# Projection phase of a transformer block on one core: output additions ahead of the maxima, other orders in the first steps and between the passes, four Q weight splits by GpSimd

## The chip, the cores and the metric

The kernel runs on one core of a Trainium2 chip. The metric is the device time of one execution in microseconds (us). The kernel before took 2551.72 us in the median of three runs (2550.61, 2551.72 and 2552.01).

## The reference, cut to what matters

The program is one layer of a block with x of 2048 tokens by 1024 features, all in float32. What the changed phase computes is this:

```
h    = rms_norm(x, norm_mix_pre)
proj = h @ w_in                      # 1024 -> 512 + 128 + 128 + 512 + 512 + 512
qa, ka, va, qd, kd, vd = split(proj)
qa, ka, qd, kd = apply_rope(...)     # heads of 64
out_a = swa_sink_attention(qa, ka, va, sinks)   # 8 query heads, 2 key heads, chunks of 64,
                                                # each chunk sees itself and the one before,
                                                # softmax with one sink per head
```

After it come the differential attention of qd, kd and vd over all earlier chunks, the output projection with its norm, and a SwiGLU block of width 2816. Those are not touched.

## The kernel before, in words

The program has three phases with a barrier between them: `proj_phase`, `diff_attn` and `out_proj_and_ffn`. Only `proj_phase` is changed.

The phase walks over tiles of 128 tokens in 33 steps, `i = 0` to `32` (`PASS` is 32, `TILES` is 16). Steps 0 to 15 are the first pass. In it tile i is scaled, turned (transposed), and multiplied by the weights of the windowed attention's Q, of its K and V together ("kv"), and of the differential attention's V ("v"); the windowed attention itself follows tile by tile with a lag. Steps 16 to 31 are the second pass, where the same tiles are turned again and multiplied by the weights of the differential attention's K ("dk") and Q ("dq"). These weights take the place of the first ones in SBUF.

Every float32 operand of a product is split into a high part (rounded, made by ScalarE) and a low part (the rest, made by VectorE), and three products are added: high by high, high by low, low by high. A weight piece is 128 rows of one weight. Pieces 16 to 23 are V's, 24 to 31 dk's and 32 to 39 dq's. `weights_hi` (L473, ScalarE) makes the high part, scaled by the norm's gain, and `weights_lo` (L613, VectorE) the low part out of the raw piece and the high part. SyncE loads a piece when the low part of the piece eight before it is done.

The order of the work is written out by hand: each engine has one instruction stream and takes it strictly in order, and semaphores tie the streams together. In step i of the first pass the streams hold, in this order:

- TensorE: `turn_x(i+1)` (L791); `project` q of tile i (L804); `score(i-1)` (L836); `attend(i-3)` (L860); `project` kv of tile i; `turn_a(i-2)`, first half (L847), the transposes of the probabilities; `turn_q(i)` (L812); `project` v of tile i; `turn_a(i-2)`, second half; `turn_k(i)` (L818).
- VectorE: `turned_lo(i+1)` (L604); `rope_q(i)` (L622, L626); `maxima(i-1)`, which writes the mask with eight memsets (L666; four in tile 0), reduces the scores to maxima (L670) and makes bias and gap (L673 to L676); `add_o(i-3)` (L716, L718, four additions that empty the two output banks); `rope_k(i)`; `scale_x(i+2)` (L598); low parts of the probabilities (L706), of q (L691 to L694) and of k; `recips(i-1)`.
- ScalarE: `turned_hi(i+1)` (L462); `square(i+2)` (L451); `copy_o(i-3)` (L531, L532); `exps(i-1)`, first half (L491), which waits for the gap of L676; `copy_v(i)` (L516), which waits for `rope_k(i)`; high parts of the probabilities (L523) and of q (L500 to L503); `exps(i-1)`, second half; `copy_dv(i)` (L538); the rest.
- GpSimd: `rotate_q(i)` (L387); `split_v(i-2)`; `rotate_k(i)`; `rstd_of(i+2)`; `scale_probs(i-1)` (L408). In the second pass `rotate_d` (L402) takes the place of the rotations.

PSUM has eight banks, and the table `BANK` with `order` says which use follows which in a bank. TensorE waits before it writes into a bank until the use before has been read out. Three entries matter here. kv and v of one tile share bank 6, and kv counts as read out when `copy_v` is done (`"kv": (v_copied, ...)`). The two halves of `attend`'s output stand in banks 5 and 4, and `turn_a`'s first half follows in them when `add_o` is done. Bank 4 holds also q and dk, and `attend`'s second half follows when the rope of q or dk has read them.

Three places have orders of their own. In step 0 the low parts of pieces 16 to 19 come last on VectorE, and in step 1 pieces 20 to 23 come before `rope_k(1)`. In step 1, TensorE runs v of tile 0, `turn_x(2)` and v of tile 1. In step 15 the pieces 24 to 31 are split, and in step 16, before VectorE's rope of dk, the pieces 32 to 39.

Of the kernel before, what the change touches and what calls it, by code (L numbers as in the profile page):

```python
# [22 lines left out]
F32 = mybir.dt.float32  # L23
F32R = mybir.dt.float32r
BF16 = mybir.dt.bfloat16
ALU = mybir.AluOpType
# [7 lines left out]
KC = D // P  # L34
# [133 lines left out]
def proj_phase(nc, x, w_in, g_pre, sinks, rope, swa_t, q_s, k_s, v_s):  # L168
# [7 lines left out]
             [("v", c, WQ, DW) for c in range(KC)]  # L176
    FIRST = {"q": 0, "kv": KC, "v": 2 * KC, "dk": 3 * KC, "dq": 4 * KC}

    order = [("x", 0, 0), ("x", 0, 1)]
# [16 lines left out]
    with ExitStack() as ctx:  # L196
# [45 lines left out]
        w_loaded = [m.sem(f"w_loaded{n}") for n in range(RAW)]  # L242
        w_hi_done, w_lo_done = m.sem("w_hi_done"), m.sem("w_lo_done")
        consts_loaded, consts_made, zeroed = m.sem("consts_loaded"), m.sem("consts_made"), m.sem("zeroed")
# [46 lines left out]
        def attending(t):  # L291
            return 0 <= t < TILES

        with nc.Block() as block:
# [76 lines left out]
            def _(pool):  # L371
# [40 lines left out]
                def split_v(t):  # L412
                    q = t % 2
                    pool.wait_ge(v_copied, t + 1)
                    if t >= 1:
# [5 lines left out]
                        .then_inc(v_split, 1)  # L421

                pool.memset(probs[:, 0, :, P:2 * P], 0.0).then_inc(zeroed, 1)
                pool.memset(probs[:, 1, :, 0:HD], 0.0).then_inc(zeroed, 1)
                rstd_of(0)
                rstd_of(1)
                for i in range(PASS):
                    u = i - TILES
                    if u >= 0:
                        rotate_d("k", u)  # L430
                    else:
                        rotate_q(i)
                    if attending(i - 2):
                        split_v(i - 2)
                    if i < TILES:
                        rotate_k(i)
                    if i + 2 < PASS:
                        rstd_of(i + 2)
                    if attending(i - 1):
                        scale_probs(i - 1)  # L440
                    if u >= 0:
                        rotate_d("q", u)

            @block.scalar
            def _(act):
# [108 lines left out]
                for i in range(PASS + 1):  # L554
                    u = i - TILES
                    if i + 1 < PASS and i != 1:
                        turned_hi(i + 1)
                    if i + 2 < PASS:
                        square(i + 2)
                    if i == TILES - 1:  # L560
                        weights_hi(3 * KC, 4 * KC)
                    if i == TILES:
                        weights_hi(4 * KC, 5 * KC)
                    if attending(i - 3):
                        copy_o(i - 3)
                    if attending(i - 1):
                        exps(i - 1, (0, 1))
                    if i < TILES:
                        copy_v(i)
# [24 lines left out]
            def _(dve):  # L594
# [61 lines left out]
                def maxima(t):  # L656
# [6 lines left out]
                    for j in range(4):  # L663
                        dve.wait_ge(scored, 4 * t + j + 1)
                        for lo, cs in chunks_hidden(t):
                            last = dve.memset(scores(j)[lo:lo + HD, :, cs, :], NEG)  # L666
                        last.then_inc(masked, 1)
                    for j in range(4):
                        dve.wait_ge(masked, 4 * t + j + 1)
                        last = dve.tensor_reduce(top[:, q, 2 * j:2 * j + 2], scores(j)[:, :, chunks_kept(t), :], AX.XY, ALU.max)  # L670
# [63 lines left out]
                for i in range(PASS + 1):  # L734
                    u = i - TILES
                    if i + 1 < PASS and i != 1:
                        turned_lo(i + 1)
                    if i == TILES:
                        weights_lo(4 * KC, 5 * KC)
                    if i < TILES:  # L740
                        rope_q(i)
                    elif i < PASS:
                        rope_d("k", u)
                    if i == 1:
                        weights_lo(5 * KC // 2, 3 * KC)
                        rope_k(i)
                    if attending(i - 1):
                        maxima(i - 1)
                    if i == TILES - 1:
                        weights_lo(3 * KC, 7 * KC // 2)  # L750
                    if attending(i - 3):
                        add_o(i - 3)
                    if i < TILES and i != 1:
                        rope_k(i)
                    if i + 2 < PASS:
                        scale_x(i + 2)
                    if attending(i - 2):
                        lo_a(i - 2, (0, 1))
                    if i < TILES:
                        lo_q(i)  # L760
                    elif u >= 1:
                        lo_d("q", u - 1)
                    if i == TILES - 1:
                        weights_lo(7 * KC // 2, 4 * KC)
                    if attending(i - 1):
# [9 lines left out]
                    elif i < PASS:  # L775
                        lo_d("k", u)
                    if i == 0:
                        weights_lo(2 * KC, 5 * KC // 2)

            @block.tensor  # L780
            def _(pe):
# [13 lines left out]
                def project(n, kind, k, region, width, done):  # L795
                    q = n % 2
                    b = free(kind, k)
                    for c in range(KC):
                        if kind in ("q", "dk") and c % 4 == 0:
                            pe.wait_ge(xt_lo_done, 2 * n + c // 4 + 1)  # L800
                        if k == 0:
                            pe.wait_ge(w_lo_done, FIRST[kind] + c + 1)
                        for j, (lhs, rhs) in enumerate(((xt_hi, w_hi), (xt_hi, w_lo), (xt_lo, w_hi))):
# [1758 lines left out]
```

## Time and profile before

| what | value |
| --- | --- |
| median of 3 runs | 2551.72 us |
| the profiled execution's own time | 2547.37 us |
| its span, first to last instruction | 2545.6 us |
| TensorE busy | 2375.7 us (93%) |
| VectorE busy | 1631.0 us (64%) |
| ScalarE busy | 1202.0 us (47%) |
| GpSimd busy | 682.6 us (27%) |
| mean granted TensorE clock | 0.978 |

Busy time is summed over all stages, so it doesn't tell which wait is worth something; that is read stage by stage. The granted clock is a share of full speed, where 1.00 stands for 2.4 GHz and 0.50 for 1.2 GHz. Matmuls are pipelined, so their shown ends overlap with the start of the next.

### The profile page before, as it was taken

What the parts mean: (1) busy time and instruction counts of PE and PEld (TensorE: products, weight loads), DVE (VectorE), ACT (ScalarE), POOL (GpSimd) and SP (SyncE); (2) the same over time, 40 slices, a digit from 0 to 9 for tenths busy, and PEclk for the clock granted to TensorE, in tenths of its full rate; (3) what the DMA queues carried; (4) which work ended last, traced back from release to release, by engine and by line L of the source; (5) the groups of instructions that cost most, each with busy time, mean ns of one, the idle gap of its engine ahead of it and who ended that gap; (6) DMA issues with size and microseconds to landing.
All of it is one profiled execution on the core that took longest, in us unless ns stands there. A gap on an engine that the chain in (4) does not pass through costs nothing.

```text
span 2545.6 us, 36648 instructions
## 1 busy us (share of the span) xinstructions
PE 2375.7 (93%) x11796; PEld 1978.0 (78%) x11796; DVE 1631.0 (64%) x3093; ACT 1202.0 (47%) x2731; POOL 682.6 (27%) x810
## 2 busy tenths in 40 slices
PE   7999997996888888799999999999999999999997
PEld 5888876885777677577778888888888888888886
DVE  5677776554898888533565545557786565464867
ACT  5555564332666666533453333335454333334444
POOL 1233322221575665445421111110000111111001
PEclk9999998998999999899999999999999999999999
DMA  5111122334232231466663233256674223226773
GB/s 175 47 55 49 52 80 76 135 135 154 74 103 77 72 88 36 161 191 228 204 211 114 96 106 110 78 182 223 229 266 154 100 100 112 100 85 240 240 264 143
DMA packets 222361, 340.08 MB, mean 134 GB/s; under 512 B 20576, under 2 KB 119904, under 8 KB 220384
## 3 DMA queue, kind: packets, MB, share of 16 engines
q1 hardware_dynamic: 222176, 337.86, 39.9%
q8 instruction: 86, 1.41, 0.2%
q14 instruction: 99, 0.81, 0.1%
HBM read 234.50 MB, written 103.28 MB: 133 GB/s over the span
## 4 chain that ended last, share of the span: by engine, by line
PE 52%; DVE 2%; POOL 2%; issue 1%; DMA 1%; ACT 1%; SPq 0%; POOLq 0%; ACTq 0%; DVEq 0%
PE ff_psum L2458 32%; PE ff_psum L2482 16%; PE ff_psum L1736 4%; PE ff_psum L1750 1%; DVE op_y_norm L1665 0%; DMA ff_ring<-in_w_down_dram 0%; DVE op_h_row L1673 0%; POOL op_mt_lo L1521 0%; POOL op_odd L1558 0%; POOL op_odd L1555 0%; ACT op_odd L1620 0%; DMA ff_hop<-hop_s 0%; DMA op_w_raw<-in_w_out_dram 0%; DVE ff_y L2422 0%; DVE ff_a_lo L2215 0%
## 5 line engine op out<-in xcount | busy, mean ns | idle before, releaser
L2458 PE MATMUL ff_psum<-ff_hop,ff_a_hi 128*128 128x512 f32 x2464 | 760.0, 390 | 5.2 <-DVE ff_hop L2222 2.9
L2458 PEld LDWEIGHTS ff_psum<-ff_hop,ff_a_hi 128*128 128x128 f32 x2464 | 462.7, 188 | 102.4 <-issue 6.6
L2458 PE MATMUL ff_psum<-ff_hop,ff_a_lo 128*128 128x512 f32 x1232 | 479.9, 390 | 0.0
L2458 PEld LDWEIGHTS ff_psum<-ff_hop,ff_a_lo 128*128 128x128 f32 x1232 | 231.7, 188 | 48.4
L2482 PE MATMUL ff_psum<-ff_a_hi 128*128 128x512 f32 x616 | 239.8, 389 | 0.3 <-DVE ff_a_lo L2215 0.3
L2482 PE MATMUL ff_psum<-ff_a_hi,ff_a_lo 128*128 128x512 f32 x616 | 239.6, 389 | 0.0
L2482 PE MATMUL ff_psum<-ff_a_lo,ff_a_hi 128*128 128x512 f32 x616 | 239.6, 389 | 0.0
L1221 ACT ACTIVATE da_probs<-da_psum,da_bias 128x512 f32<-128x512 f32 (+3 forms) x320 | 195.9, 621 | 73.6 <-DVE da_bias L1273 60.7
L2088 ACT ACTIVATE ff_a_hi<-ff_w_raw 128x512 fp32r<-128x512 f32 x220 | 137.9, 629 | 193.9 <-PE ff_psum L2458 190.5
L2215 DVE TENSOR_TENSOR ff_a_lo<-ff_w_raw,ff_a_hi 128x512 fp32r<-128x512 f32 x220 | 163.4, 744 | 90.6 <-ACT ff_a_hi L2088 90.6
L2043 POOL TENSOR_TENSOR ff_go<-ff_go 128x512 f32<-128x512 f32 x22 | 28.4, 1291 | 655.2 <-DVE ff_go L2296 635.0
L1267 DVE TENSOR_REDUCE da_tops<-da_psum 128x1 f32<-128x512 f32 (+3 forms) x288 | 173.7, 619 | 26.4 <-PE da_psum L1328 22.0
L2215 DVE TENSOR_TENSOR ff_a_lo<-ff_ring,ff_a_hi 128x512 fp32r<-128x512 f32 x220 | 151.0, 696 | 45.7 <-ACT ff_a_hi L2088 45.7
L2088 ACT ACTIVATE ff_a_hi<-ff_ring 128x512 fp32r<-128x512 f32 x220 | 130.7, 622 | 96.8 <-PE ff_psum L2482 82.5
L1351 PE MATMUL da_psum<-da_values,da_at 128*128 (+1 forms) x1088 | 149.4, 280 | 18.5 <-ACT da_at L1229 10.8
L1351 PEld LDWEIGHTS da_psum<-da_values,da_at 128*128 128x128 f32 x1088 | 138.4, 193 | 34.3 <-issue 19.2
L1328 PE MATMUL da_psum<-da_keys,da_q_hl 128*128 (+3 forms) x320 | 139.9, 440 | 26.0 <-DMA da_keys<-k_s 15.5
L2482 PEld LDWEIGHTS ff_psum<-ff_a_hi 128*128 128x128 f32 x616 | 115.6, 188 | 24.8 <-DVE ff_a_lo L2215 0.7
L2482 PEld LDWEIGHTS ff_psum<-ff_a_lo,ff_a_hi 128*128 128x128 f32 x616 | 115.6, 188 | 24.0
L2482 PEld LDWEIGHTS ff_psum<-ff_a_hi,ff_a_lo 128*128 128x128 f32 x616 | 115.6, 188 | 23.9
L2266 DVE TENSOR_TENSOR ff_s<-ff_psum,ff_s 128x512 f32<-128x512 f32 x66 | 45.6, 691 | 120.8 <-ACT ff_s L2098 84.8
L1328 PE MATMUL da_psum<-da_keys,da_q_lh 128*128 (+3 forms) x320 | 120.3, 378 | 0.0
(230 smaller groups left out, 5000.4 us busy)
## 6 DMA issues: line engine op xcount, KB each, us to landing
g_s<-ff_go SPq DMA_DIRECT2D x154, 256.0 KB, 2.0
ff_ring<-g_s SPq DMA_DIRECT2D x154, 256.0 KB, 2.8
ff_ring<-in_w_down_dram SPq DMA_DIRECT2D x132, 256.0 KB, 3.1
ff_w_raw<-in_w_gate_dram SPq DMA_DIRECT2D x44, 512.0 KB, 3.6
ff_w_raw<-in_w_up_dram SPq DMA_DIRECT2D x44, 512.0 KB, 3.9
pp_x<-in_x_dram SPq DMA_DIRECT2D x32, 512.0 KB, 4.3
ff_hop<-hop_s SPq DMA_DIRECT2D x14, 1024.0 KB, 7.8
hop_s<-op_odd SPq DMA_DIRECT2D x8, 1280.0 KB, 5.5
```

The lines of the kernel that those rows point to most:

```text
L1221: act.activation(probs[:, q, m, 4 * P * c:4 * P * c + w], ps[:, b, 0:w], ACT.Exp, bias=bias[:, r, m:m + 1], accum_out=sums[:, r, m, c:c + ...
L1267: top = dve.tensor_reduce(tops[:, r, m, c:c + 1], ps[:, b, 0:w], AX.X, ALU.max)
L1328: last = pe.matmul(ps[:, b, 0:w], stack[:, s % Q_SLOTS, m, :], keys[:, bass.ds(h, 1), m, 4 * P * c:4 * P * c + w].squeeze(1), start=(j == ...
L1351: last = pe.matmul(ps[:, O_BANK, 0:VD], at[:, n % A_SLOTS, j, :], values[:, bass.ds(h, 1), 4 * c + j, :].squeeze(1), start=(c == 0 and j = ...
L1736: last = pe.matmul(self.ps[:, self.y_banks.bank("y", k, n), :], lhs[:, q, c, :], rhs[n][:, c, :], start=(c == 0 and j == 0), stop=(c == KC ...
L1750: last = pe.transpose(self.ps[:, self.h_bank(k, n), j * P:(j + 1) * P], self.b.op_h_row[:, at:at + P], self.b.op_ident[:, :])
L2043: pool.tensor_tensor(go[:, S1, :], go[:, C12, :], go[:, C22, :], ALU.add).then_inc(go_made, 1)
L2088: act.activation(a_hi[:, n_ % R, :], source, ACT.Copy).then_inc(w_hi_done, 1)
L2215: dve.tensor_tensor(a_lo[:, n_ % R, :], unit_source(n_)[0], a_hi[:, n_ % R, :].bitcast(F32), ALU.subtract)\
L2266: return dve.tensor_tensor(to, ps[:, bank, :], to, ALU.add)
L2458: last = pe.matmul(ps[:, bank, :], w[:, unit % R, at], hop[i][:, h, c, :], start=(i in (0, 1, 6) and c == 0 and x_ == 0), stop=(c == 3 and ...
L2482: last = pe.matmul(ps[:, bank, :], g[:, unit % R, at], w[:, (unit + 1) % R, :], start=(i in (0, 1, 6) and c == 0 and x_ == 0), stop=(c == ...
```

## The change

It has these parts, all in `proj_phase`:

- In `maxima(t)` the additions `add_o(t-2)` now stand between the mask's memsets and the reductions. So they come before the maxima in each step from 3 to 16. In steps 17 and 18 `add_o` stands where it did.
- In step 0 VectorE does `rope_q(0)` before `turned_lo(1)`. All eight V pieces are split in step 1, after `rope_q(1)` and `rope_k(1)`. On ScalarE `copy_v(1)` comes before the exponentials of step 1.
- In step 15 ScalarE makes the high parts of pieces 24 to 27 before `copy_o` and those of 28 to 31 behind it. VectorE does the low parts of 24 to 27 after `rope_k(15)`, and those of 28 to 31 before `lo_q(15)`.
- In step 16 ScalarE makes the high parts of pieces 32 to 39 before `square(18)`. The low parts of 32 to 35 are made by GpSimd (a scaling of the raw piece in place, then a subtraction), ahead of `rotate_d("k", 0)`. VectorE makes those of 36 to 39 after the maxima.

```diff
+    BY_POOL = KC // 2
@@ gpsimd
+                def weights_lo_of_q():
+                    for k in range(BY_POOL):
+                        n = FIRST["dq"] + k
+                        _, c, _, width = pieces[n]
+                        raw = w_raw[:, n % RAW, 0:width]
+                        pool.wait_ge(w_hi_done, n + 1)
+                        pool.tensor_scalar(raw, raw, g_col[:, c:c + 1], 1.0, ALU.mult, ALU.mult).then_inc(w_pool_scaled, 1)
+                        pool.wait_ge(w_pool_scaled, k + 1)
+                        pool.tensor_tensor(w_lo["v"][:, c, 0:width], raw, w_hi["v"][:, c, 0:width].bitcast(F32), ALU.subtract)\
+                            .then_inc(w_pool_lo_done, 1)
...
+                    if i == TILES:
+                        weights_lo_of_q()
                     if u >= 0:
                         rotate_d("k", u)
@@ scalar
                     if i + 1 < PASS and i != 1:
                         turned_hi(i + 1)
+                    if i == TILES:
+                        weights_hi(4 * KC, 5 * KC)
                     if i + 2 < PASS:
                         square(i + 2)
                     if i == TILES - 1:
-                        weights_hi(3 * KC, 4 * KC)
-                    if i == TILES:
-                        weights_hi(4 * KC, 5 * KC)
+                        weights_hi(3 * KC, 7 * KC // 2)
                     if attending(i - 3):
                         copy_o(i - 3)
+                    if i == TILES - 1:
+                        weights_hi(7 * KC // 2, 4 * KC)
+                    if i == 1:
+                        copy_v(i)
                     if attending(i - 1):
                         exps(i - 1, (0, 1))
-                    if i < TILES:
+                    if i < TILES and i != 1:
                         copy_v(i)
@@ maxima
                         last.then_inc(masked, 1)
+                    if attending(t - 2):
+                        add_o(t - 2)
                     for j in range(4):
@@ vector
-                    if i + 1 < PASS and i != 1:
+                    if 1 < i < PASS - 1:
                         turned_lo(i + 1)
-                    if i == TILES:
-                        weights_lo(4 * KC, 5 * KC)
                     if i < TILES:
                         rope_q(i)
                     elif i < PASS:
                         rope_d("k", u)
+                    if i == 0:
+                        turned_lo(1)
                     if i == 1:
-                        weights_lo(5 * KC // 2, 3 * KC)
                         rope_k(i)
+                        weights_lo(2 * KC, 3 * KC)
                     if attending(i - 1):
                         maxima(i - 1)
+                    if attending(i - 3) and not attending(i - 1):
+                        add_o(i - 3)
+                    if i == TILES:
+                        weights_lo(FIRST["dq"] + BY_POOL, 5 * KC)
+                    if i < TILES and i != 1:
+                        rope_k(i)
                     if i == TILES - 1:
                         weights_lo(3 * KC, 7 * KC // 2)
-                    if attending(i - 3):
-                        add_o(i - 3)
-                    if i < TILES and i != 1:
-                        rope_k(i)
                     if i + 2 < PASS:
                         scale_x(i + 2)
                     if attending(i - 2):
                         lo_a(i - 2, (0, 1))
+                    if i == TILES - 1:
+                        weights_lo(7 * KC // 2, 4 * KC)
                     if i < TILES:
                         lo_q(i)
...
-                    if i == 0:
-                        weights_lo(2 * KC, 5 * KC // 2)
@@ tensor, project
-                        if k == 0:
-                            pe.wait_ge(w_lo_done, FIRST[kind] + c + 1)
+                        if kind == "dq" and k == 0 and c < BY_POOL:
+                            pe.wait_ge(w_pool_lo_done, c + 1)
+                        elif k == 0:
+                            pe.wait_ge(w_lo_done, FIRST[kind] + c + 1 - (BY_POOL if kind == "dq" else 0))
```

## Rows read from the trace of the kernel before

**Rows 1.** The page, its first line: the span.
```profile
span 2545.6 us, 36648 instructions
```

**Rows 2.** TensorE's waits, 0 to 600 us: total, times, longest.
```profile
PE pp_psum L847 <- DVE pp_o_sum L718: 21.8, 22, 4.2
PE pp_psum L860 <- DVE pp_part_s L626: 8.5, 3, 7.4
PE pp_psum L804 <- ACT pp_v_raw L516: 7.2, 2, 5.7
```

**Rows 3.** Windows, one per step (3, 9, 10, 15, 16): length, busy by engine, PEclk, DMA.
```profile
87.70:112.22 24.52, 21.86 (x123) 18.99 (x122) 16.64 (x41) 13.08 (x37) 6.84 (x7) 0.93 0.16 49
...
222.21:245.16 22.95, 21.20 (x127) 18.45 (x126) 16.64 (x41) 13.09 (x37) 6.84 (x7) 1.00 0.18 52
245.16:266.49 21.33, 21.14 (x127) 18.44 (x126) 15.24 (x40) 12.77 (x37) 6.83 (x7) 1.00 0.20 57
355.12:382.32 27.20, 22.80 (x127) 19.82 (x126) 21.94 (x48) 17.19 (x43) 6.84 (x7) 0.94 0.35 104
382.32:405.77 23.45, 12.98 (x58) 10.26 (x57) 14.26 (x35) 12.18 (x33) 6.06 (x6) 0.71 0.10 32
```

**Rows 4.** Timeline of TensorE in step 9: start, us, engine, line, tiles.
```profile
230.35 0.63 PE L847 MATMUL pp_psum<-pp_ident,pp_probs 128*128 128x128 f32 x4 [1.56 <-DVE pp_o_sum L718]
...
232.06 0.50 PE L804 MATMUL pp_psum<-pp_wv_hi,pp_xt_hi 128*128 128x512 f32 x1
```

**Rows 5.** Timeline of VectorE in step 9.
```profile
223.68 2.95 DVE L666 MEMSET pp_psum<- 64x256 f32 x8
...
229.26 0.16 DVE L676 TENSOR_TENSOR pp_gap<-pp_sink,pp_top 128x8 f32<-128x8 f32 x1
229.34 0.41 DVE L716 TENSOR_TENSOR pp_o_sum<-pp_psum,pp_o_tmp 64x256 f32<-64x256 f32 x1
...
230.69 0.43 DVE L718 TENSOR_TENSOR pp_o_sum<-pp_psum,pp_o_tmp 64x256 f32<-64x256 f32 x1
```

**Rows 6.** Timeline of ScalarE in step 9.
```profile
229.45 0.47 ACT L491 ACTIVATE pp_probs<-pp_psum,pp_bias 128x256 f32<-128x256 f32 x1 [2.73 <-DVE pp_gap L676]
...
231.73 0.28 ACT L516 ACTIVATE pp_v_raw<-pp_psum 128x128 f32<-128x128 f32 x1 [0.35 <-DVE pp_rot_ks L626]
```

**Rows 7.** Timeline of VectorE in step 8, which began at 200.87.
```profile
204.13 1.87 DVE L670 TENSOR_REDUCE pp_top<-pp_psum 128x2 f32<-128x384 f32 x4
...
206.32 0.16 DVE L676 TENSOR_TENSOR pp_gap<-pp_sink,pp_top 128x8 f32<-128x8 f32 x1
```

**Rows 8.** Timeline of ScalarE in step 8.
```profile
205.01 0.38 ACT L532 ACTIVATE pp_o_tmp<-pp_psum 64x256 f32<-64x256 f32 x1
...
208.79 0.28 ACT L516 ACTIVATE pp_v_raw<-pp_psum 128x128 f32<-128x128 f32 x1 [0.56 <-DVE pp_rot_ks L626]
```

**Rows 9.** Windows after two of TensorE's stalls, columns as in rows 3.
```profile
44.24:49.30 5.06, 5.06 (x12) 4.04 (x13) 2.75 (x4) 2.18 (x4) 0.00 (x0) 0.50 0.00 0
...
417.90:421.30 3.40, 3.40 (x15) 3.01 (x16) 2.81 (x5) 1.82 (x4) 0.01 (x1) 0.51 0.02 5
```

**Rows 10.** Timeline of TensorE in step 17: the stall before 417.90.
```profile
417.85 1.93 PE L847 MATMUL pp_psum<-pp_ident,pp_probs 128*128 128x128 f32 x8 [1.80 <-DVE pp_o_sum L718]
```

**Rows 11.** Groups of GpSimd's instructions by line and form: count, busy us, mean ns.
```profile
L1184 POOL TENSOR_SCALAR da_probs<-da_probs,da_factor 128x512 f32<-128x512 f32 x72 | 57.1, 793 | 100.3 <-DVE da_factor L1285 99.8 <-issue 0.5
L402 POOL TENSOR_TENSOR pp_rot<-pp_part_c,pp_part_s 128x512 f32<-128x512 f32 x32 | 41.4, 1293 | 163.2 <-DVE pp_part_s L626 163.2
```

**Rows 12.** Timeline of VectorE, steps 0 and 1: V pieces split.
```profile
31.90 2.74 DVE L613 SCALAR_TENSOR_TENSOR pp_wv_lo<-pp_w_raw,pp_g_col,pp_wv_hi 128x512 fp32r<-128x512 f32 x4
...
35.94 3.74 DVE L613 SCALAR_TENSOR_TENSOR pp_wv_lo<-pp_w_raw,pp_g_col,pp_wv_hi 128x512 fp32r<-128x512 f32 x4
```

**Rows 13.** Timeline of GpSimd in step 1: an addition beside V pieces' splits.
```profile
36.10 1.70 POOL L387 TENSOR_TENSOR pp_rot<-pp_part_c,pp_part_s 128x512 f32<-128x512 f32 x1 [9.52 <-DVE pp_part_s L626]
```

**Rows 14.** Timeline of ScalarE in step 1.
```profile
52.39 0.60 ACT L538 ACTIVATE pp_dv<-pp_psum 128x512 f32<-128x512 f32 x1 [5.94 <-PE pp_psum L804]
```

More of the change, by code:

```diff
@@ L242, in proj_phase @@
         w_loaded = [m.sem(f"w_loaded{n}") for n in range(RAW)]
-        w_hi_done, w_lo_done = m.sem("w_hi_done"), m.sem("w_lo_done")
+        w_hi_done, w_lo_done, w_pool_scaled, w_pool_lo_done = (
+            m.sem(n) for n in ("w_hi_done", "w_lo_done", "w_pool_scaled", "w_pool_lo_done"))
         consts_loaded, consts_made, zeroed = m.sem("consts_loaded"), m.sem("consts_made"), m.sem("zeroed")
@@ L762, in _ @@
                         lo_d("q", u - 1)
-                    if i == TILES - 1:
-                        weights_lo(7 * KC // 2, 4 * KC)
                     if attending(i - 1):
```

## The prediction

> **What bounds the kernel now.** I read three views in this order. The page gives the span of 2545.6 us [rows 1]. The list of TensorE's waits up to 600 us shows where the phase loses time: 21.8 us in 22 waits of the first half of `turn_a` (L847) for `add_o`, 8.5 us in three waits of `attend` (L860) for a rope, 7.2 us in two waits of `project` (L804) for `copy_v` [rows 2]. The reader is to see that these are small sums in a phase that is otherwise full of matmuls. Then windows that run from one rope of q to the next give the length of a step: the odd step 9 takes 22.95 us with TensorE busy for 21.20 (1.75 idle), the even step 10 takes 21.33 with 21.14 (0.19 idle), step 3 24.52, step 15 27.20 and step 16 23.45 [rows 3]. TensorE sets the pace, and a change is worth what it does to TensorE's stalls in such a step. Odd steps attend to the even tiles, whose masks and maxima are larger.
>
> **Additions ahead of the maxima: what goes.** In step 9, which begins at 222.21, TensorE waits 1.56 us for `add_o` before `turn_a` [rows 4]. The additions run from 229.34 to 231.12, 1.78 us, behind the gap at 229.26 [rows 5]. Moved to the end of the memsets (223.68 + 2.95 = 226.63) they are done before kv is, and that stall goes.
>
> **What comes in its place.** All that is behind the additions in VectorE's stream moves back by their length: the reductions, the gap, and so the exponentials on ScalarE, which start right at the gap (229.45) [rows 6]. Queued behind the first half of the exponentials on ScalarE is `copy_v`. ScalarE was idle for 0.35 us before it, waiting for `rope_k`, so the exponentials ended at 231.73 - 0.35 = 231.38 [rows 6]. `rope_k` stays where it is in time, since additions and maxima only swap. Now the exponentials end at 231.38 + 1.78 = 233.16, and `copy_v` at about 233.16 + 0.02 + 0.28 = 233.46. Who waits for `copy_v`? v, which goes into the bank that kv leaves. v starts at 232.06 now, 0.05 us after `copy_v` ends at 232.01 [rows 4, 6]. This is the point of the case: the way over the late transposes and the way over `copy_v` already end within hundredths of each other, and that v can stand behind `copy_v` is seen in the two waits of 7.2 us [rows 2]. So v starts at about 233.5 instead of 232.06: an odd step gets 1.45 us longer, and its idle of 1.75 us becomes 3.2, nearly all in one piece before v.
>
> In an even step the memsets are done by about 204.15, where the reductions begin [rows 7], but the second half of `copy_o` is ready only at 205.01 + 0.38 = 205.39 [rows 8]. The last two additions (0.86, as in [rows 5]) end at about 206.25, and the reductions start 2.1 us later than at 204.13. ScalarE had 0.56 us of idle before `copy_v` [rows 8]. So v starts 2.1 - 0.5 = 1.6 us later, and the idle of 0.19 becomes 1.8.
>
> What stands behind v goes along: from v to the next rope is 245.16 - 232.06 = 13.1 us of TensorE's work [rows 3, 4], and the second exponentials, `recips` and `scale_probs` keep their distance to `copy_v`. Nothing gives the time back. Steps 5, 7, 9, 11 and 13: 5 x 1.45 = 7.3 us. Steps 4, 6, 8, 10, 12 and 14: 6 x 1.6 = 9.6 us. Step 3 becomes an odd step of the new kind with the clock loss that it has already (below): 22.95 + 1.45 + 1.7 = 26.1 against 24.52, +1.6. Together +18.5 us. Bounds: at worst the 0.35 and 0.56 us of `copy_v` don't help (+23). At best nothing stands behind `copy_v` and all of TensorE's waits for the additions go (-13: the 21.8 less 4.2, about 3 and 1.8 us of steps 15, 16 and 17 [rows 2, 10]). I take +18.5, because each link has its row.
>
> **The clock.** Step 3 ran at a mean of 0.93 and step 15 at 0.94: 24.52 x 0.07 = 1.7 us lost in each [rows 3]. After the stall in step 1 TensorE worked 5.06 us at 0.50, that is at 1.2 GHz instead of 2.4, and behind a stall of only 1.80 us it ran from 417.90 to 421.30 at 0.51 [rows 9, 10]. Steps whose largest stall is 1.56 us ran at 1.00 [rows 3, 4]. The new stall of an odd step, 3.2 us, is well above both; that of an even step, 1.8 us, equals the smallest that has cost something. I take 1.7 us for each of five odd steps (8.5) and for half of the even ones (3 x 1.7 = 5.1): +13.6, between 0 and 18.7.
>
> **Step 15.** Four of the eight splits no longer stand between the maxima and `add_o`, and the others come before `lo_q`, while TensorE has 13 us of v, transposes and dk to do. It becomes an odd step of the new kind, 24.4 us plus 1.7 for the clock: 26.1 against 27.20, -1.1 (-2.8 if the clock holds).
>
> **Step 16.** Before, `attend`'s second half waited for the rope of dk behind eight splits, up to 7.4 of the 8.5 us [rows 2], and the clock was 0.71 [rows 3]. Now the high parts start right after `turned_hi(17)`, in the last 5 us of step 15, and the rope is first on VectorE. The additions end 5.4 us into the step (206.25 - 200.87, as in step 8), transposes follow (0.63 for a group of four [rows 4]), and dq starts at about 5.9. It needs pieces 32 to 35 from GpSimd. The scaling is bounded by GpSimd's 0.79 us for a tensor_scalar and its 1.29 for a two-input operation of the same 128x512 [rows 11]; I take 0.79 as the same kind, so a piece takes 0.79 + 1.29 = 2.1 us and four 8.3 (10.3 at the upper bound). `scale_probs(14)` holds GpSimd until about half a microsecond before the step, so the fourth piece is there at 7.9. TensorE needs 0.63 us or a little more per piece (three of the 12 matmuls of 5.06 us at half clock [rows 9]) and wants it at 7.8. VectorE's four, 2.7 us behind the maxima [rows 12], come from 8.5 to 10.6, and TensorE wants the first at 8.5. With a few tenths of waiting dq ends at about 12.2 (14.2 at the upper bound) instead of 23.45: -11.2, between -12 and -9. The rotations and the rstd of tile 18 queue behind GpSimd's splits until about 10.5; `turn_x(18)`, which needs them, stands behind dq, so TensorE covers them, with 2 us to spare.
>
> The Trainium skill speaks against this part (SBUF — State Buffer, "SBUF: two separate sides"): VectorE operations with two SBUF inputs and GpSimd operations take turns at a shared port pair, as an exclusive lock. The trace agrees: four V splits took 2.74 us alone but 3.74 beside one addition of GpSimd, which took 1.70 instead of 1.29 [rows 11 to 13]. By that rule VectorE's four splits and small operations of `maxima(15)` wait for GpSimd; the third rival prices it.
>
> **Steps 0 and 1.** With the V splits behind both ropes, q's rotation comes earlier, and v of tile 0 runs from about 36 us, before the exponentials. ScalarE waited 5.94 us for that product before `copy_dv(0)` [rows 14]; this wait goes, and the second exponentials and `turn_x(2)` come 5.9 us earlier. The maxima stay at about 42 us, since the same eight splits (2.74 + 3.74 [rows 12]) come before them. TensorE then idles for some 6 us before `turn_x(2)`, and v of tile 1 starts at the low clock: 5.06 / 2 = 2.5 us lost [rows 9]. -5.9 + 2.5 = -3.5, between -6 and 0.
>
> **Sum.** 18.5 + 13.6 - 1.1 - 11.2 - 3.5 = +16.3 us. I take 2 us off for stalls that pass without a drop of the clock, and forecast +14. The profiled execution took 2547.4 us (1.8 around its span), so it would take 2561. The median of the runs shown is 4.3 us above this execution; on it the forecast is 2551.7 + 14, written 2566. Its own range, from the terms, is 2557 to 2576.
>
> **Rivals.** First, the clock holds in the steps. For: only a few drops are in the trace, and 1.56 us did nothing. Against: 1.80 us was enough once. Then 18.5 - 1.7 - 2.8 - 11.2 - 3.5 = -0.7 us: 2551. It decides between slower and same.
>
> Second, the other side: v waits for `copy_v` no longer than now, because in step 9 it was held by TensorE's own work after the late `turn_a` and ScalarE has slack that I don't see. Then the waits for the additions go: -13 in steps 3 to 14, -4.2 in step 15, -11.2 in step 16, -3.5 at the start, -32 us: 2520. It decides if `copy_v` ends less than 8.1 us after the rope of an odd step (9.85 now, less 1.75 idle). For it: 22 waits name the additions and two name `copy_v` [rows 2]. Against it: the one stream puts `copy_v` behind the exponentials, and its end is 0.05 us before v today.
>
> Third, GpSimd and VectorE block each other in step 16: each of VectorE's four splits waits 1.0 us for a GpSimd operation, as one did in [rows 12, 13], and dq ends 4 us later: 2570.
>
> **Numbers.** Forecast 0.60, first rival 0.18, second 0.11, third 0.11. A difference below 0.2% (5.1 us) can't be told from none. Faster (below 2546.6): the second and 0.03 of the first, 0.14. Same: the rest of the first and 0.02 from the low end of the forecast, 0.17. Slower: 0.69. The range 2548 to 2576 holds the forecast, the third rival and most of the first.
>
> **What would show it.** Right: TensorE's 21.8 us for the additions shrink to a few, and waits of `project` for `copy_v` appear in each step from 3 to 15, 3 us in odd and 1.8 in even ones; an odd step takes 24.4 us or more, an even one 22.9; odd steps show a clock under 1.00; step 16 takes about 12 us. Wrong: steps 4 to 14 are no longer than 22.95 and 21.33, or step 16 stays above 15 us.

## The result, and the profile after

The changed kernel takes 2561.18 us in the median of five executions (2560.55 to 2563.68). The kernel before, run beside it, takes 2550.61 (2548.22 to 2552.01). The ratio is 1.0043, with a 95% interval from 1.0033 to 1.0054: slower by 10.6 us. The two profiled executions lie further apart, 2563.26 against 2547.37, 15.9 us. The balance below is made against those two.

First the page of the changed kernel.

```profile
span 2561.5 us, 36652 instructions
...
PE 2383.4 (93%) x11796; PEld 1984.5 (77%) x11796; DVE 1631.1 (64%) x3089; ACT 1203.3 (47%) x2731; POOL 694.0 (27%) x818
```

The span is 15.9 us longer [rows 1]. The same 11796 matmuls keep TensorE busy 7.7 us longer (2375.7 before), and the other 8 us are idle. Busy time grows with a slow clock too, so these two numbers don't yet separate stall from clock. TensorE's waits up to 610 us say where (total, times, longest):

```profile
PE pp_psum L827 <- ACT pp_v_raw L531: 37.6, 14, 4.0
...
PE pp_psum L812 <- ACT pp_probs L506: 6.1, 1, 6.1
PE pp_psum L870 <- DVE pp_o_sum L739: 3.7, 3, 2.6
PE pp_psum L883 <- DVE pp_part_s L645: 1.1, 2, 0.5
```

Against [rows 2]: the waits for the additions fell from 21.8 us to 3.7 and those of `attend` for a rope from 8.5 to 1.1. In their place stand 14 waits of `project` (now L827) for `copy_v` (now L531), 37.6 us instead of 7.2. One stall has been swapped for another at a different place, and the new one is longer. How much longer a step is shows in the windows from rope to rope, columns as in [rows 3]. They are steps 2 to 4, 7 to 10, 15 and 16.

```profile
62.66:83.28 20.62, 19.17 (x119) 16.95 (x118) 13.56 (x36) 11.06 (x33) 6.79 (x7) 1.00 0.07 20
83.28:109.93 26.65, 22.56 (x123) 19.31 (x122) 16.77 (x41) 12.99 (x37) 6.84 (x7) 0.87 0.14 45
109.93:134.51 24.58, 22.61 (x127) 19.68 (x126) 15.42 (x40) 12.57 (x37) 6.83 (x7) 0.93 0.17 49
...
185.12:209.51 24.39, 21.00 (x127) 18.45 (x126) 16.77 (x40) 13.00 (x37) 6.83 (x7) 1.00 0.18 50
209.51:232.53 23.02, 21.05 (x127) 18.45 (x126) 15.42 (x40) 12.58 (x37) 6.84 (x7) 1.00 0.18 52
232.53:259.59 27.06, 23.67 (x127) 20.38 (x126) 16.78 (x41) 12.99 (x37) 6.83 (x7) 0.87 0.15 45
259.59:284.16 24.57, 22.60 (x127) 19.58 (x126) 15.42 (x40) 12.57 (x37) 6.83 (x7) 0.93 0.16 49
...
383.21:407.63 24.42, 21.04 (x127) 18.46 (x126) 22.10 (x49) 21.32 (x51) 8.55 (x8) 1.00 0.44 135
407.63:421.69 14.06, 11.99 (x67) 9.37 (x66) 12.86 (x32) 8.17 (x29) 11.13 (x13) 1.00 0.07 20
```

Two kinds of lengthening have to be separated here. Where the clock is 1.00, an odd step takes 24.4 us with 3.39 idle (step 7) and an even one 23.02 with 1.97 idle (step 8). That is the stall alone. Where it is 0.93 or 0.87, TensorE is busy for 22.6 or 23.7 us with the same work, and the step is 1.6 or 2.7 us longer again. That is the clock.

The stall can be followed in step 9, which begins at 232.53. VectorE, ScalarE and TensorE in one timeline:

```profile
234.00 2.95 DVE L685 MEMSET pp_psum<- 64x256 f32 x8
...
236.86 0.41 DVE L737 TENSOR_TENSOR pp_o_sum<-pp_psum,pp_o_tmp 64x256 f32<-64x256 f32 x1
...
238.67 2.48 DVE L691 TENSOR_REDUCE pp_top<-pp_psum 128x2 f32<-128x512 f32 x4
...
241.47 0.16 DVE L697 TENSOR_TENSOR pp_gap<-pp_sink,pp_top 128x8 f32<-128x8 f32 x1
...
241.66 0.48 ACT L506 ACTIVATE pp_probs<-pp_psum,pp_bias 128x256 f32<-128x256 f32 x1 [4.61 <-DVE pp_gap L697]
...
243.49 0.29 ACT L531 ACTIVATE pp_v_raw<-pp_psum 128x128 f32<-128x128 f32 x1
...
243.83 0.80 PE L827 MATMUL pp_psum<-pp_wv_hi,pp_xt_hi 128*128 128x512 f32 x1 [3.39 <-ACT pp_v_raw L531]
```

The additions stand ahead of the reductions and are done early. The gap comes 8.94 us into the step instead of 7.05 [rows 5], `copy_v` 10.96 instead of 9.52 [rows 6], v 11.30 instead of 9.85 [rows 4]. `copy_v` no longer has idle time of its own in front: it goes straight behind the last exponential.

The clock behind three of these stalls (3.39, 1.97 and 3.39 us, in steps 9, 10 and 11), in windows of the same kernel:

```profile
244.10:249.20 5.10, 5.10 (x13) 3.94 (x14) 3.60 (x7) 4.92 (x15) 0.00 (x0) 0.50 0.00 0
...
269.50:272.90 3.40, 3.40 (x9) 2.71 (x10) 2.09 (x4) 3.34 (x7) 0.00 (x0) 0.58 0.07 21
...
295.90:301.00 5.10, 5.10 (x24) 4.16 (x23) 3.60 (x7) 4.75 (x14) 0.00 (x0) 1.00 0.00 0
```

Behind the 3.39 us of step 9 TensorE runs at 1.2 GHz for 5 us, 13 matmuls where step 11 does 24 in the same time. Step 11 has the same stall and loses nothing.

Step 16, which begins at 407.63, in one timeline of all engines:

```profile
413.95 1.30 POOL L433 TENSOR_TENSOR pp_wv_lo<-pp_w_raw,pp_wv_hi 128x512 fp32r<-128x512 f32 x1
...
415.21 1.29 POOL L404 TENSOR_TENSOR pp_rot<-pp_part_c,pp_part_s 128x512 f32<-128x512 f32 x1
415.31 1.22 DVE L696 TENSOR_SCALAR pp_bias<-pp_top 128x8 f32<-128x8 f32 x1
...
416.67 2.92 DVE L632 SCALAR_TENSOR_TENSOR pp_wv_lo<-pp_w_raw,pp_g_col,pp_wv_hi 128x512 fp32r<-128x512 f32 x4
...
417.47 0.50 PE L827 MATMUL pp_psum<-pp_wv_hi,pp_xt_hi 128*128 128x512 f32 x1 [0.93 <-DVE pp_wv_lo L632]
```

GpSimd has its fourth piece 7.6 us into the step. VectorE's are 1 us later than they could be: the bias, 8 values in each partition, takes 1.22 us instead of the 0.17 that it took in step 9. It starts 0.1 us after GpSimd's rotation of dk and ends with it. dq waits 0.93 us for that and ends 12.9 us into the step.

In step 1 the wait of `copy_dv(0)` [rows 14] is gone, and TensorE idles before `turn_x(2)`:

```profile
47.83 1.94 PE L812 MATMUL pp_psum<-pp_ident,pp_x 128*128 128x128 f32 x8 [6.08 <-ACT pp_probs L506]
```

The balance of the phase, after less before, profiled executions, from the windows of all steps:

| stretch | us |
| --- | --- |
| up to step 2 (begins at 62.66, was 67.09) | -4.4 |
| step 3 | +2.1 |
| odd steps 5, 7, 9, 11, 13 (128.94, was 114.82) | +14.1 |
| even steps 4 to 14 (144.34, was 128.08) | +16.3 |
| step 15 (24.42, was 27.20) | -2.8 |
| step 16 up to the end of dq (12.90, was 23.25) | -10.4 |
| from there to the phase's last `turn_d` | +0.9 |
| sum | +15.8 |

### The profile page after: what moved, and what is told of

Same layout as the page of the kernel before. It is cut to its first block, busy times and chain, and to the rows that moved or that the text cites. A ratio compares the mean times of both kernels' runs of the same rounds, so it can differ in the third digit from the quotient of the medians.

```text
span 2561.5 us, 36652 instructions
## 1 busy us (share of the span) xinstructions
PE 2383.4 (93%) x11796; PEld 1984.5 (77%) x11796; DVE 1631.1 (64%) x3089; ACT 1203.3 (47%) x2731; POOL 694.0 (27%) x818
## 4 chain that ended last, share of the span: by engine, by line
PE 52%; POOL 2%; DVE 2%; issue 1%; DMA 1%; ACT 1%; SPq 0%; POOLq 0%; ACTq 0%; DVEq 0%
PE ff_psum L2481 32%; PE ff_psum L2505 15%; PE ff_psum L1759 4%; PE ff_psum L1773 0%; DVE op_y_norm L1688 0%; DMA ff_ring<-in_w_down_dram 0%; DVE op_h_row L1696 0%; POOL op_mt_lo L1544 0%; POOL op_odd L1581 0%; POOL op_odd L1578 0%; ACT op_odd L1643 0%; DMA ff_hop<-hop_s 0%; DVE ff_y L2445 0%; DMA op_w_raw<-in_w_out_dram 0%; POOL op_y_rstd L165 0%
## 5 line engine op out<-in xcount | busy, mean ns | idle before, releaser
L1374 PE MATMUL da_psum<-da_values,da_at 128*128 (+1 forms) x1088 | 149.0, 280 | 17.4 <-ACT da_at L1252 10.4
L1351 PE MATMUL da_psum<-da_keys,da_q_hl 128*128 (+3 forms) x320 | 139.8, 439 | 25.9 <-DMA da_keys<-k_s 15.6
L827 PE MATMUL pp_psum<-pp_wv_hi,pp_xt_hi 128*128 128x512 f32 x256 | 111.2, 434 | 38.6 <-ACT pp_v_raw L531 37.6
L2505 PEld LDWEIGHTS ff_psum<-ff_a_hi 128*128 128x128 f32 x616 | 115.7, 188 | 24.4 <-DVE ff_a_lo L2238 0.5
```

Source lines behind the costliest of these rows:

```text
L827: last = pe.matmul(ps[:, b, 0:width], lhs[:, q, c, :], rhs[region][:, c, 0:width], start=(c == 0 and j == 0), stop=(c == KC - 1 and j == 2))
L1351: last = pe.matmul(ps[:, b, 0:w], stack[:, s % Q_SLOTS, m, :], keys[:, bass.ds(h, 1), m, 4 * P * c:4 * P * c + w].squeeze(1), start=(j == ...
L1374: last = pe.matmul(ps[:, O_BANK, 0:VD], at[:, n % A_SLOTS, j, :], values[:, bass.ds(h, 1), 4 * c + j, :].squeeze(1), start=(c == 0 and j = ...
L2505: last = pe.matmul(ps[:, bank, :], g[:, unit % R, at], w[:, (unit + 1) % R, :], start=(i in (0, 1, 6) and c == 0 and x_ == 0), stop=(c == ...
```

## The experiments

The theory was: (a) the additions lengthen each step from 3 to 14, because `copy_v` stands behind the exponentials on ScalarE and v behind `copy_v`; (b) part of the loss is the clock; (c) the other parts of the change gain. The rivals were that the loss comes from another part of the change, that `copy_v` isn't what v waits for, and for (c) that GpSimd's splits are what gains in step 16. In diffs "-" is the kernel that is edited.

**One part alone: the additions, in the kernel before.**

```diff
                         last.then_inc(masked, 1)
+                    if attending(t - 2):
+                        add_o(t - 2)
                     for j in range(4):
...
-                    if attending(i - 3):
+                    if attending(i - 3) and not attending(i - 1):
                         add_o(i - 3)
```

> The kernel before with one part of the change alone: add_o ahead of the reductions in steps 3 to 16. Theory (v waits for copy_v, copy_v for the exponentials, these for the maxima, and the additions push all of them back): steps 3 to 14 become as long as in the changed kernel, some 32 us more in all; step 15 hardly moves (27 us), since its splits stay where they were; step 16 some 1 to 2 us shorter. About 2581 us, 30 us above before. TensorE's waits for copy_v: some 3.4 us in odd and 2.0 in even steps. Rival (the loss comes from the new orders of steps 0, 1, 15 and 16 or from GpSimd's splits): within 5 us of before or faster, since the 21.8 us of waits for the additions go.

Measured: 2580.74 us (2579.41 to 2583.52), the kernel before 2550.05 there, ratio 1.0125 [1.0110, 1.0141]. TensorE's largest wait, and its windows of steps 8 to 11:

```profile
PE pp_psum L806 <- ACT pp_v_raw L516: 45.2, 15, 5.7
```

```profile
213.70:236.69 22.99, 21.03 (x127) 18.46 (x126) 15.41 (x41) 12.54 (x37) 6.83 (x7) 1.00 0.18 52
236.69:263.77 27.08, 23.71 (x127) 20.46 (x126) 16.76 (x41) 12.96 (x37) 6.83 (x7) 0.87 0.15 44
263.77:288.33 24.56, 22.60 (x127) 19.61 (x126) 15.41 (x40) 12.54 (x37) 6.83 (x7) 0.93 0.16 49
288.33:312.72 24.39, 21.02 (x127) 18.46 (x126) 16.76 (x41) 12.97 (x37) 6.83 (x7) 1.00 0.16 49
```

The steps have the lengths of the changed kernel, and even the clock falls in the same ones. This part alone costs 30.7 us, three times the loss of the whole change. Steps 15 and 16 together take 50.9 us against 50.7 before, so the 1 to 2 us less that were expected there didn't come.

**The whole change without that part** (the edit above, undone in the changed kernel).

> The changed kernel with add_o put back behind the maxima, all else as changed. Theory: steps 4 to 14 are back at 22.95 (odd) and 21.33 us (even), the start keeps its 4.4 us of gain, step 15 becomes an odd step of the old kind (about 23 us), step 16 loses some of its gain because the additions come later (14 to 15 us). About 2533 us, 17 us below before and 28 below the changed kernel. Rival (the start and the handoff cost something by themselves, hidden behind the additions): not below 2545 us.

Measured: 2531.82 us (2530.84 to 2532.85), ratio 0.9929 [0.9916, 0.9943]. It was run once more, on another chip:

> The kernel of e2_additions_back once more, on one chip with its pair without GpSimd's splits, since the two were measured on different chips and stood 2.7 us apart. Theory: about 2532 us, within 1.5 us of the pair. Rival: 2.7 us below the pair.

There it took 2535.09 (2533.84 to 2535.39) beside 2550.16, ratio 0.9939 [0.9926, 0.9952], 3 us above the time expected. Steps 9 and 10, here from the first of the two runs, are those of before:

```profile
216.82:239.76 22.94, 21.20 (x127) 18.46 (x126) 16.63 (x41) 13.08 (x37) 6.83 (x7) 1.00 0.18 53
239.76:261.12 21.36, 21.17 (x127) 18.44 (x126) 15.23 (x40) 12.78 (x37) 6.83 (x7) 1.00 0.19 57
```

All else gains 15 to 18 us. The two halves, +30.7 and -18.2, add up to +12.5 (+15.6 with the second run), where the change measured +10.6.

**`copy_v` ahead of the exponentials, in the changed kernel.**

```diff
-                    if i == 1:
+                    if i < TILES:
                         copy_v(i)
                     if attending(i - 1):
                         exps(i - 1, (0, 1))
-                    if i < TILES and i != 1:
-                        copy_v(i)
```

> The changed kernel with copy_v ahead of the first exponentials on ScalarE in every step; the additions stay ahead of the maxima, so maxima and exponentials stay as late as in the changed kernel or get some 0.6 us later. Theory (only the way over copy_v costs): v follows rope_k by 0.3 us, at about 10.0 us into an odd step and 8.7 into an even one instead of 11.3 and 9.9; steps of 23.1 and 21.8 us; fewer drops of the clock. About 2538 us, 23 us below the changed kernel. Rival (the late exponentials cost by other ways: the second half of turn_a, turn_x, scale_probs): the steps stay at 24 us or more, 2555 us or above.

Measured: 2536.67 us (2534.78 to 2539.76), ratio 0.9951 [0.9935, 0.9966]. TensorE's largest wait and steps 9 to 11:

```profile
PE pp_psum L825 <- ACT pp_v_raw L531: 20.0, 14, 2.7
```

```profile
219.24:243.87 24.63, 22.61 (x127) 19.62 (x126) 16.79 (x40) 12.96 (x37) 6.84 (x7) 0.93 0.17 49
243.87:265.71 21.84, 21.02 (x127) 18.45 (x126) 15.51 (x40) 12.42 (x37) 6.84 (x7) 1.00 0.18 56
265.71:288.81 23.10, 21.08 (x127) 18.44 (x126) 16.80 (x40) 12.85 (x37) 6.83 (x7) 1.00 0.17 52
```

The third line is step 11. Steps 5, 7, 11 and 13 take 23.1 us at 1.00, so an odd step is 1.3 us shorter than in the changed kernel and an even one 1.2. The stall is not gone: `copy_v` still waits for `rope_k`, which stands behind the reductions. 24.5 us come back by moving one short instruction, some 14 of them as shorter stalls in steps 4 to 14 and the rest mostly as a clock that holds: of steps 3 to 15 only 3 and 9 still run below 1.00.

**The first steps alone, in the kernel before** (`turned_lo(1)` behind `rope_q(0)`, all V splits behind `rope_k(1)`, `copy_v(1)` first).

```diff
...
                     if i == 1:
-                        weights_lo(5 * KC // 2, 3 * KC)
                         rope_k(i)
+                        weights_lo(2 * KC, 3 * KC)
...
-                    if i == 0:
-                        weights_lo(2 * KC, 5 * KC // 2)
```

> The kernel before with the new orders of steps 0 and 1 alone. Theory (the wait of copy_dv(0) and the second exponentials for v of tile 0 goes, part of it comes back as a slow clock after a 6 us stall before turn_x(2)): step 2 begins 4.4 us earlier, steps from 2 on unchanged: 2546 us, between -6 and -2. Rival (the drops of the clock later on shift and eat it): within 1 us of before.

Measured: 2543.89 us (2540.60 to 2546.16, 11 executions), ratio 0.9977 [0.9968, 0.9986]. Step 2 begins at 61.56 instead of 67.09. This part is worth 5.5 us in the profile and 6.2 in the medians, a little more than the -6 to -2 expected.

**GpSimd's splits given to VectorE.** The kernel without the early additions again, with all eight low parts of pieces 32 to 39 on VectorE.

```diff
-    BY_POOL = KC // 2
+    BY_POOL = 0
```

> The kernel of e2_additions_back, with all eight Q weight splits of step 16 on VectorE behind the maxima and additions, none on GpSimd. Theory: the Q product starts with the first of VectorE's pieces, about 8.5 us into step 16, and each piece (0.69 us) comes as fast as TensorE uses it (0.70), so the product ends within 1 us of where it does with GpSimd's four; GpSimd's part of the change is worth 0 to 1 us: 2531 to 2533 us. Rival (GpSimd's splits are what makes the handoff short): four pieces later, 2.7 us or more, 2535 us or above.

Measured: 2534.48 us (2532.42 to 2537.24) beside 2550.95 on one chip, ratio 0.9935 [0.9922, 0.9949]. That is above the 2531 to 2533 expected, and 2.7 us above the 2531.82 of the kernel with GpSimd's splits, as the rival has it. The two were measured on different chips, so both were run again on one. On the chip where the kernel with GpSimd's splits took 2535.09 us:

> The kernel of e5_no_gpsimd once more, beside e9_additions_back_again. Theory: its handoff is as long in the trace, so within 1.5 us of that kernel. Rival (GpSimd's splits are worth 2.7 us): 2.7 us above it.

It took 2533.62 (2530.56 to 2537.74), 1.5 us below its pair and within the scatter of its own runs, so the 2.7 us of the rival aren't there. Sharing the splits between two engines gives nothing that can be measured. The gain between the passes comes from the order alone: without GpSimd's splits the kernel is still 16.5 us below the one before, of which the first steps are worth 6.2. VectorE in step 16 shows why sharing doesn't help. First with GpSimd's splits, then without:

```profile
378.37 1.26 DVE L694 TENSOR_SCALAR pp_bias<-pp_top 128x8 f32<-128x8 f32 x1
...
381.42 4.00 DVE L632 SCALAR_TENSOR_TENSOR pp_wv_lo<-pp_w_raw,pp_g_col,pp_wv_hi 128x512 fp32r<-128x512 f32 x4
```

```profile
379.25 0.17 DVE L694 TENSOR_SCALAR pp_bias<-pp_top 128x8 f32<-128x8 f32 x1
...
381.22 5.39 DVE L632 SCALAR_TENSOR_TENSOR pp_wv_lo<-pp_w_raw,pp_g_col,pp_wv_hi 128x512 fp32r<-128x512 f32 x8
```

Four splits beside GpSimd take 4.00 us, eight without it 5.39. Together with the bias, GpSimd's help buys 0.3 us of VectorE's time.

**What the stall needs to go.** In the changed kernel `rope_k` comes right behind the additions, ahead of the reductions. `copy_v` and `hi_q` come ahead of the exponentials, `lo_q` ahead of the low parts of the probabilities.

```diff
                     if attending(t - 2):
                         add_o(t - 2)
+                    if 1 < t + 1 < TILES:
+                        rope_k(t + 1)
                     for j in range(4):
...
-                    if i == 1:
+                    if i < TILES:
                         copy_v(i)
+                    if 1 < i < TILES:
+                        hi_q(i)
                     if attending(i - 1):
                         exps(i - 1, (0, 1))
...
```

> The changed kernel with three orders more, in steps 2 to 15: rope_k right behind the additions and ahead of the reductions, copy_v and the high parts of q ahead of the first exponentials on ScalarE, the low parts of q ahead of those of the probabilities on VectorE. Theory: copy_v ends 7.5 us into a step, before TensorE wants it at 8.1, the exponentials start at 10.1 and end before the second half of turn_a, so both kinds of steps take about 21.2 us at full clock: 12 us of 1.75 and step 3's stall less than the steps of before, and the start, step 15 and step 16 keep their gains: about 2516 us, 35 below before. Rival (the exponentials, now 0.6 us later still, hold the second half of turn_a or turn_x): steps of 22.5 us or more, 2530 us or above.

Measured: 2517.69 us (2515.42 to 2519.74), ratio 0.9867 [0.9852, 0.9882]. Steps 9 and 10:

```profile
207.94:229.25 21.31, 21.16 (x127) 18.41 (x126) 16.70 (x41) 12.94 (x37) 6.84 (x7) 1.00 0.18 57
229.25:250.14 20.89, 20.89 (x127) 18.41 (x126) 15.42 (x41) 12.51 (x37) 6.83 (x7) 1.00 0.20 58
```

And the timeline of VectorE, ScalarE and TensorE in step 9, around the start of v:

```profile
214.56 0.29 DVE L641 TENSOR_TENSOR pp_rot_kc<-pp_psum,pp_rope 128x128 f32<-128x128 f32 x1 [0.52 <-PE pp_psum L831]
...
215.15 0.28 ACT L531 ACTIVATE pp_v_raw<-pp_psum 128x128 f32<-128x128 f32 x1 [2.70 <-DVE pp_rot_ks L645]
...
215.59 0.48 PE L831 MATMUL pp_psum<-pp_wv_hi,pp_xt_hi 128*128 128x512 f32 x1
```

`copy_v` ends at 215.43 and v starts at 215.59, with no idle in its row. An even step has none at all, an odd one 0.15 us. This version is 1.3% faster than the kernel before and 14 to 17 us faster than the two runs with the additions behind the maxima. How much of that is due to the early additions isn't shown: three orders were changed at once, and no run has them with the additions at their old place. What speaks for the additions is that TensorE's waits for `add_o` are gone from steps 3 to 14 here, while in the kernel with the additions behind the maxima they are still 20.7 us in 24 waits over the phase. The same with `BY_POOL = 0`:

> The kernel of e6_all_early with all eight Q weight splits of step 16 on VectorE, none on GpSimd. Theory (GpSimd's splits only move work that the Q product doesn't wait for): within 1.5 us of e6_all_early, 2516 to 2519 us. Rival (they are worth the time of four pieces): 2520 us or above.

It took 2517.97 us (2516.02 to 2520.21) beside 2550.16, on another chip than its pair, ratio 0.9876 [0.9862, 0.9891]. Here too no worth of GpSimd's splits can be measured.

**The clock's share.** In the changed kernel TensorE does the four transposes of `turn_q` five times in each step from 3 to 15. The extra ones write the same result over it.

```diff
-                    for j in range(4):
+                    for j in 5 * list(range(4)) if t >= 3 else range(4):
```

> The changed kernel with the four transposes of turn_q done five times over in steps 3 to 15, into the same bank from the same data: some 1.7 us of TensorE work that nobody needs, in the place of the stall before v. Theory (the stalls cost twice, once as idle time and once as a slow clock behind them): the stall shrinks to 1.7 us in odd and 0.3 us in even steps, no step gets longer, and the clock stays at 1.00, so the 13 to 14 us that steps 3 to 14 lost to the clock come back: about 2548 us, although TensorE does more work. Rival (the clock's drops come from elsewhere or cost nothing net): 2559 us or above.

Measured: 2551.01 us (2546.84 to 2552.70, 11 executions) beside 2550.95, ratio 0.9997 [0.9988, 1.0006]. Steps 9 and 10, and the start of v in step 9:

```profile
227.09:251.52 24.43, 22.80 (x143) 20.20 (x142) 16.75 (x40) 12.97 (x37) 6.84 (x7) 1.00 0.17 50
251.52:274.51 22.99, 22.77 (x143) 20.20 (x142) 15.42 (x41) 12.54 (x37) 6.84 (x7) 1.00 0.18 53
```

```profile
238.37 0.50 PE L827 MATMUL pp_psum<-pp_wv_hi,pp_xt_hi 128*128 128x512 f32 x1 [1.63 <-ACT pp_v_raw L531]
```

With 1.75 us more work in each of 13 steps the kernel is 10.2 us faster. The end of the stall is set by `copy_v`, so the transposes lie inside it, and every step from 3 to 15 runs at 1.00. Their lengths are those of the changed kernel's steps in which the clock held. So the clock costs the changed kernel some 10 us in the medians. In the profiled executions it is more: steps 3 to 15 take 308.7 us instead of 324.4, 15.6 us less; put down to the clock in the changed kernel are 2.2 us of step 3 and 13.2 of steps 4 to 14. A part of the rest is that this execution began step 2 at 64.31 us and not at 62.66, with the same orders up to there. The run doesn't tell whether the clock holds for the shorter idle time (1.63 us before v in step 9 instead of 3.39) or for the transposes themselves, since both came together.

## Why the prediction was right, point by point

**The whole.** Slower was forecast, by 14 us and to 2566 us. The kernel is slower by 10.6 and takes 2561.18, inside the range of 2548 to 2576. The mechanism was the one forecast. That the sum of the terms came so close owes something to luck, as the clock's parts show.

**Additions and maxima.** The forecast was 24.4 us for an odd step and 22.9 for an even one, with v behind `copy_v`. Where the clock held they took 24.4 and 23.02, 1.43 and 1.68 us more than before, where 1.45 and 1.6 stood in the sum. These are 7.1 us in five odd and 10.1 in six even steps (forecast 7.3 and 9.6). The link on which it hung, that `copy_v` queues behind the exponentials and v behind it, is shown from both sides: the additions alone make the stall, moving `copy_v` alone shortens it, and moving `rope_k` as well, with the splits of q, ends it. The second rival (2520, v waits no longer than now) is refuted in the form in which it was put. Its lesson holds all the same: with a short chain to v the kernel takes 2518.

**The clock.** Forecast +13.6, measured 7.0 us in the odd and 6.2 in the even steps, 13.2. The total was right, its parts only roughly, and that they cancel is luck. Not all five odd steps lost but three (5, 9 and 13), two of them 2.7 us instead of 1.7. Of six even steps four lost 1.6 instead of three 1.7. Step 3, with a stall of 4.0 us, lost 2.2, so it grew by 2.1 and not 1.6. In step 15 the clock held, and the step fell by 2.8 us, the value that stood in brackets, instead of 1.1. The first rival (2551, the clock holds) is refuted by the changed kernel. The kernel with the extra transposes, where it does hold, took the 2551 us of that rival.

The 2 us that were taken off for stalls without a drop were a guess on top of a sum that had already let half the even steps off.

**Step 16.** dq started 5.9 us into the step and GpSimd's fourth piece was there at 7.6, as reckoned (5.9 and 7.9). dq ended at 12.9 instead of 12.2, so the gain was 10.4 us and not 11.2. (The 11.2 set the end of dq against the whole step before, 23.45 us; dq ended at 23.25. The whole step takes 14.06 us now, not the 12 that the prediction gave as a sign.) The term that was too small is the start of VectorE's splits. It rested on the maxima taking their usual time, but the bias waited 1 us for GpSimd. The third rival had the right cause, the two engines in each other's way, at another operation and a quarter of its price: 1 us where it said 4. VectorE's four splits, on which it laid the 4 us, took 2.92 us instead of 2.74. That GpSimd's work is the cause is shown by taking it away: the same bias takes 1.22, 1.26 and 1.17 us in three kernels with GpSimd's splits (the changed one, the one without early additions, the one with `rope_k` early too), each time ending with the GpSimd operation beside it, and 0.17 us in the three runs with `BY_POOL = 0`. The Trainium skill (SBUF — State Buffer, "SBUF: two separate sides") gives the shared port pair for a whole instruction to whichever starts first, a GpSimd operation or one of VectorE that has two SBUF inputs or runs in a two-port mode. The trace agrees with a block for the whole instruction: the bias ended with GpSimd's rotation, 1.22 us after its own start. The bias has only one SBUF input, so it would have to be in a two-port mode, which the trace doesn't show. VectorE's additions, which read one operand from PSUM, ran beside GpSimd's splits at their usual 0.42 to 0.43 us.

**Steps 0 and 1.** -4.4 us against a forecast of -3.5. The wait of 5.9 us went as forecast and `turn_x(2)` came at 47.83 instead of 53.83, with 6.08 us of idle before it. The low clock behind it lasted for less than the 5.06 us of [rows 9]:

```profile
47.83:51.60 3.77, 3.77 (x13) 3.39 (x14) 3.10 (x6) 1.85 (x7) 1.90 (x1) 0.50 0.49 106
```

That is 1.9 us lost and not 2.5. From `turn_x(2)` to the end of v of tile 1 it took 8.15 us against 6.60 before, 1.55 more, and 6.0 less 1.55 is the 4.4. Behind step 16 the stall of `turn_a` grew from 1.80 [rows 10] to 2.60 us, 0.9 us with what follows, which the prediction didn't have.

**The sum.** The terms gave +16.3, the profiled executions differ by 15.9. The medians differ by only 10.6. That is not a fault of a term: the changed kernel's profiled execution is 2.1 us above its median and that of before 3.2 below its own. A part of such differences lies in the first steps: the ten runs with the new orders of steps 0 and 1 begin step 2 anywhere between 61.56 and 65.10 us in their profiles, and the two profiles of the kernel with neither early additions nor GpSimd's splits are 3.3 us apart, of which 2.6 lie before step 2. So the -4.4 us of the start has an uncertainty of this size. What makes executions of one kernel differ I leave open. The forecast of +14 lies between the two differences.

**What stays open.** Why the clock falls in steps 3 to 6, 9, 10, 13 and 14 and holds in 7, 8, 11, 12 and 15, although the changed kernel's stalls before v are 3.38 or 3.39 us in all odd steps from 5 to 15 and 1.97 us in all even ones (step 3 has 4.04). The kernel with the additions alone shows the same pattern, so it doesn't belong to one execution. With `copy_v` first, step 9 ran at 0.93 and step 11 at 1.00, both with 2.02 us idle. No run here takes it apart.

## What to carry to other kernels

Before an operation is moved forward on an engine, list what moves back by its length, and follow that over the other engines to what TensorE waits for: here additions put in front of the maxima cost 30.7 us, and with the same order the kernel was 33 us faster than before once the short releasing operations (`rope_k`, `copy_v`) stood ahead of the long ones. Reckon a stall twice, once for its length and once for the clock behind it: of the 30.4 us that steps 4 to 14 lost, 13.2 were the clock.

## What the runs showed of the hardware that was not expected

- An operation of VectorE on 128x8 values took 1.22 and 1.26 us instead of 0.17, when it started beside a GpSimd operation of 128x512 (1.29 and 1.26 us). It ended with that operation both times, so here the length of the other engine's operation counted, not its own.
- Four splits beside GpSimd's work took 2.92 to 4.00 us, while eight alone took 5.39. Half the work given to GpSimd (2.0 us a piece there) bought nothing.
- Extra transposes inside a stall made the kernel 10.2 us faster, with the clock at 1.00 in each step from 3 to 15.
- Stalls of about 2 us (even steps) were followed by 1.2 GHz in four steps of six, and stalls of 3.4 us (odd steps from 5 to 15) in three of six.
